# Per-head rows of a mixer-and-experts layer spread over the partitions by broadcast transfers instead of one-hot products

## The reference, cut to what matters

```
# mLSTM, 4 heads: causal weights from a cumulated gate row b and an input gate row
D = where(causal, b[..., :, None] - b[..., None, :] + ig[..., None, :], -inf)
m_t = maximum(inter, max(D, -1)); Dw = exp(D - m_t[..., None]); iw = exp(inter - m_t)
# gated delta rule, 8 heads: a decay row gc and a factor row beta
gc  = cumsum(g, -1)
gam = exp(where(causal, gc[..., :, None] - gc[..., None, :], -inf))
a_mat = where(strict, beta[..., :, None] * gam * einsum('bhcld,bhcsd->bhcls', k, k), 0)
sol = triangular_solve(eye + a_mat, rhs);  p = gam * einsum(q, k)
qg  = q * exp(gc)[..., None]
```

## Time and profile before

| what | value |
|---|---|
| three runs | 1386.42, 1386.41, 1384.55 us, median 1386.41 us |
| the profiled execution's own time | 1386.72 us |
| its span in the trace | 1384.9 us |
| TensorE busy | 1309.3 us, 95% of the span |
| VectorE busy | 334.1 us, 24% |
| ScalarE busy | 178.0 us, 13% |
| moved by DMA | 460.64 MB, mean 333 GB/s |

### The profile page before, as it was taken

How to read it: one execution, slowest core, us unless ns; L and a number is a source line. 1 busy time by engine, 2 the same in 40 slices (tenths; PEclk the granted TensorE clock), 3 DMA queues, 4 the chain that set the end, 5 groups by cost and what they waited for, 6 DMA issues and landing times.

```text
span 1384.9 us, 18396 instructions
## 1 busy us (share of the span) xinstructions
PE 1309.3 (95%) x7510; PEld 710.6 (51%) x7510; DVE 334.1 (24%) x724; ACT 178.0 (13%) x271; POOL 9.7 (1%) x17
## 2 busy tenths in 40 slices
PE   7999999999999999999999989899998989989895
PEld 6888888888886443443433324233332423333241
DVE  3847473122133111112011020110201011020113
ACT  1331622011001100101000100010010001001000
POOL 0110000000000000000000000000000000000000
PEclk9999999999999999999999999999999999999998
DMA  6533323323796999999999999999999999999995
GB/s 234 182 122 107 110 81 116 128 87 133 296 352 231 370 421 421 422 422 422 422 421 422 421 422 422 422 422 422 422 421 422 421 422 422 422 422 422 422 422 209
DMA packets 72274, 460.64 MB, mean 333 GB/s; under 512 B 14096, under 2 KB 14736, under 8 KB 17584
## 3 DMA queue, kind: packets, MB, share of 16 engines
q1 hardware_dynamic: 65824, 455.24, 80.9%
q10 hardware_dynamic: 6416, 4.93, 1.2%
HBM read 458.70 MB, written 1.44 MB: 332 GB/s over the span
## 4 chain that ended last, share of the span: by engine, by line
PE 57%; SPq 21%; DMA 18%; DVE 3%; issue 2%; ACT 0%; DVEq 0%
SPq L369 21%; PE ps L483 19%; PE ps L832 16%; DMA mix<-expert_w 10%; DMA ring<-expert_w 6%; PE ps L850 4%; PE ps L501 3%; PE ps L789 3%; PE ps L777 3%; PE ps L825 3%; PE ps L724 2%; PE ps L493 1%; DMA ring<-small_w 1%; DMA mix<-x_turned 1%; DMA mix<-stream_w 1%
## 5 line engine op out<-in xcount | busy, mean ns | idle before, releaser
L832 PE MATMUL ps<-ring,mix 128*64 128x512 f32 x1536 | 343.1, 592 | 2.5 <-DMA ring<-expert_w 2.5
L483 PE MATMUL ps<-mix 128*128 128x256 f32 x1248 | 273.7, 380 | 2.2 <-DVE ring L1423 2.2
L483 PEld LDWEIGHTS ps<-mix 128*128 128x128 f32 x1248 | 235.9, 190 | 35.7 <-issue 4.1
L832 PEld LDWEIGHTS ps<-ring,mix 128*64 128x64 f32 x1536 | 108.6, 137 | 210.3 <-issue 192.5
L850 PE MATMUL ps<-ring,mix 128*64 128x512 f32 x768 | 181.2, 599 | 31.6 <-DMA ring<-expert_w 31.6
L1662 DVE TENSOR_SCALAR mix<-ps 128x512 f32<-128x512 f32 x32 | 22.1, 692 | 539.6 <-PE ps L832 539.6
L850 PEld LDWEIGHTS ps<-ring,mix 128*64 128x64 f32 x768 | 50.4, 136 | 149.1 <-issue 83.4
L832 PE MATMUL ps<-mix 128*64 128x512 f32 x512 | 116.4, 593 | 2.1 <-DMA mix<-expert_w 2.1
L1671 DVE COPY mix<-ps 128x512 f32<-128x512 f32 x32 | 22.1, 692 | 239.2 <-PE ps L841 239.2
L850 PE MATMUL ps<-mix 128*64 128x512 f32 x256 | 60.6, 601 | 12.5 <-DMA mix<-expert_w 12.5
L789 PEld LDWEIGHTS ps<-mix 128*64 128x64 f32 x1088 | 63.9, 142 | 11.0 <-issue 9.1
(11 more groups left out here) (254 smaller groups left out, 780.0 us busy)
## 6 DMA issues: line engine op xcount, KB each, us to landing
ring<-expert_w SPq DMA_DIRECT2D x288, 1024.0 KB, 26.5
mix<-expert_w SPq DMA_DIRECT2D x96, 1024.0 KB, 26.8
mix<-stream_w SPq DMA_DIRECT2D x42, 1024.0 KB, 4.8
mix<-stream_w SPq DMA_DIRECT2D x10, 512.0 KB, 4.1
mix<-x_turned SPq DMA_DIRECT2D x2, 512.0 KB, 5.9
mix<-planes ACTq DMA_DIRECT2D x1, 1024.0 KB, 9.6
mix<-x SPq DMA_DIRECT2D x2, 512.0 KB, 6.1
mix<-ln_g ACTq DMA_DIRECT2D x2, 512.0 KB, 6.3
```

The costliest lines, as they stand in the source:

```text
L483: ins = mm(o[:, m * S:(m + 1) * S], w[:, c, m * P:(m + 1) * P], rhs[:, c, :], start=(m == 0 and c == 0), stop=(c == nk - 1), skip_group_ch ...
L832: ins = mm(PS[64 * a:64 * a + 64, bank + g, :], XE[j][:, c, 64 * a:64 * a + 64], w[:, a * D + g * 512:a * D + g * 512 + 512], start=False, ...
```

## The change

The one-hot products bb, gb, gr and mr go. Three DRAM tensors are added: `rows_gb` (2 x 8 x 256), `rows_gt` (2 x 8 x 128) and `rows_m` (4 x 3 x 128). SP writes the rows there in five transfers behind the load of lx0, and reads them back, each spread over 64 or 128 partitions, in four transfers behind the load of lx1 (`EG` in two of 256 KB, `GAM` 1 MB, `ME` 768 KB) and two behind the load of ly0 (`KB`, 512 KB in all). DVE and ACT then work in place on `EG`, `KB`, `GAM` and `ME` in SBUF, where they read PSUM before. DVE multiplies KB in two instructions instead of four. The banks of later projections shift by two places in the rotation of four. The order of everything else stays.

```diff
-FILL = (("mq", "mk", "mr0", "mr1", "lg"), ...
+FILL = (("mq", "mk", "lg"), ...
...
+                if name == "lx0":
+                    sp.wait_ge(E("rows_ready"), 1)
+                    sp.wait_ge(E("rows_ready_act"), 3)
+                    sp.dma_start(rows_gb[0], RW[64:64 + GH]).then_inc(E("rows_out"), 16)
+                    sp.dma_start(rows_gb[1], RW[96:96 + GH]).then_inc(E("rows_out"), 16)
+                    sp.dma_start(rows_gt.rearrange("t h l -> h t l"), RW[64:64 + GH].rearrange("h (t l) -> h t l", t=NT)
+                                 ).then_inc(E("rows_out"), 16)
+                    sp.dma_start(rows_m[:, 0:2, :], NM[0:MH].rearrange("h (b l) -> h b l", b=2)
+                                 ).then_inc(E("rows_out"), 16)
+                    sp.dma_start(rows_m[:, 2, :], NM[0:MH, P:2 * P]).then_inc(E("rows_out"), 16)
+                if name == "lx1":
+                    sp.wait_ge(E("rows_out"), 80)
+                    for a in range(2):
+                        sp.dma_start(EG[64 * a:64 * a + 64], rows_gb[0].rearrange("(j a) s -> a j s", a=2)[a]
+                                     .partition_broadcast(64)).then_inc(E("eg_in"), 16)
+                    sp.dma_start(GAM, rows_gt.rearrange("t h l -> (t h l)").rearrange("(n q) -> n q", n=4)
+                                 .partition_broadcast(P)).then_inc(E("gam_in"), 16)
+                    sp.dma_start(ME, rows_m.partition_broadcast(P)).then_inc(E("me_in"), 16)
+                if name == "ly0":
+                    sp.wait_ge(E("gsilu"), 1)
+                    for a in range(2):
+                        sp.dma_start(KB[64 * a:64 * a + 64, :, a, :], rows_gb[1].rearrange("(j a) s -> a j s", a=2)[a]
+                                     .partition_broadcast(64)).then_inc(E("beta_in"), 16)
...  (TensorE: the loops for bb, gb, gr and mr are taken out)
...  (ScalarE)
-                full(act, f"gb{n}")
-                A(EG[:, 2 * n:2 * n + 2, :], ps(f"gb{n}").rearrange("p (c s) -> p c s", s=S), ACT.Exp
-                  ).then_inc(free(f"gb{n}"), 1)
+                act.wait_ge(E("eg_in"), 32)
+                A(EG[:, 2 * n:2 * n + 2, :], EG[:, 2 * n:2 * n + 2, :], ACT.Exp).then_inc(E("eg"), 1)
...  (VectorE)
-                    ins = tt(KB[h, 2 * n:2 * n + 2, a, :], ps(f"bb{n}")[h].rearrange("p (c s) -> p c s", s=S),
-                             KT[h, 2 * n:2 * n + 2, :], ALU.mult)
+            dve.wait_ge(E("beta_in"), 32)
+                step(tt(KB[h, :, a, :], KB[h, :, a, :], KT[h], ALU.mult))
...
+            dve.wait_ge(E("eg"), 2)
...
+            dve.wait_ge(E("gam_in"), 16)
+                    gam = GAM[:, 2 * t + h // 4, (h % 4) * P:(h % 4 + 1) * P]
+                    ins = stt(gam, gam, RC[:, t, 0, 64 + h:65 + h], CM[:, K_GTRI], ALU.subtract, ALU.add)
+                    if h % 4 == 3:
                         ins.then_inc(E("gam_arg"), 1)
...
+                dve.wait_ge(E("me_in"), 16)
+                        stt(ME[:, h, 0, :], ME[:, h, 0, :], RC[:, 0, 0, h:h + 1], CM[:, K_MTRI], ALU.add, ALU.add)
+                        ts(ME[:, h, 1, :], ME[:, h, 1, :], RC[:, 0, 0, h:h + 1], None, ALU.add)
```

More of the change, by code:

```diff
@@ L102 @@
 NB16 = P // BS
[L103 removed]
+FILL = (("mq", "mk", "lg"), ("ms00", "ms10", "ms01", "ms11", "mv0"), ("mv1",), ("mo0", "mn"),
         ("mo1", "gz0", "mt", "gz1"), ("ga00",))
@@ L145, in bank_uses @@
     p("lx2", "lx3")
-    order += [("bb0", 4), ("bb1", 5), ("gb0", 6), ("gb1", 7)]
     p("ly0")
     order += [("vt0", 4), ("vt1", 5), ("kt0", 6), ("kt1", 7)]
-    order += [(f"gr{n}", 4 + n) for n in range(4)]
     p("ly1")
@@ L343, in layer_kernel @@
         blocks = nc.dram_tensor("blocks", (3, NB16, P // NB16, BS, BS), F32, kind="Internal").ap()
+        rows_gb = nc.dram_tensor("rows_gb", (2, GH, S), F32, kind="Internal").ap()
+        rows_gt = nc.dram_tensor("rows_gt", (NT, GH, P), F32, kind="Internal").ap()
+        rows_m = nc.dram_tensor("rows_m", (MH, 3, P), F32, kind="Internal").ap()
         def diagonal(buf, g):
@@ L537, in _ @@
                 proj(f"lx{n}")
[L539 to L554, removed]
             proj("ly0")
@@ L561, in _ @@
                 many(f"kt{t}", [(j * P, j * P + P, KT[:, j, t * P:(t + 1) * P], ident) for j in range(GP)])
-            for n in range(4):
-                many(f"gr{n}", [(m * S, m * S + S, ident[:, 64 + 2 * n + m:65 + 2 * n + m].to_broadcast([P, P]), RW)
-                                for m in range(2)])
             proj("ly1")
@@ L584, in fill @@
                             many(f"lg{b}", [(k * S, k * S + S, w[:, k, b, :], XA[:, b, :]) for k in range(2)])
[L585 to L590, removed]
                     elif name[:2] == "ms":
@@ L1265, in _ @@
             dve.sem_inc(E("khat"), 1)
[L1266 to L1269, removed]
-                    ins = tt(KB[h, 2 * n:2 * n + 2, a, :], ps(f"bb{n}")[h].rearrange("p (c s) -> p c s", s=S),
-                             KT[h, 2 * n:2 * n + 2, :], ALU.mult)
-                ins.then_inc(free(f"bb{n}"), 1)
-                dve.wait_ge(free(f"bb{n}"), uses[f"bb{n}"][1])
+            dve.wait_ge(E("beta_in"), 32)
+            for a in range(2):
+                h = slice(64 * a, 64 * a + 64)
+                step(tt(KB[h, :, a, :], KB[h, :, a, :], KT[h], ALU.mult))
             dve.sem_inc(E("kb_ready"), 1)
@@ L1280, in _ @@
             conv_lru(1)
-            for n in range(2):
-                moved(dve, f"gb{n}")
+            dve.wait_ge(E("eg"), 2)
             for a in range(2):
@@ L1302, in _ @@
                 dve.wait_ge(free(f"kt{t}"), uses[f"kt{t}"][1])
+            dve.wait_ge(E("gam_in"), 16)
             for t in range(NT):
                 for h in range(GH):
[L1306 to L1313, removed]
+                    gam = GAM[:, 2 * t + h // 4, (h % 4) * P:(h % 4 + 1) * P]
+                    ins = stt(gam, gam, RC[:, t, 0, 64 + h:65 + h], CM[:, K_GTRI], ALU.subtract, ALU.add)
+                    if h % 4 == 3:
                         ins.then_inc(E("gam_arg"), 1)
-            for n in range(4):
-                dve.wait_ge(free(f"gr{n}"), uses[f"gr{n}"][1])
-            dve.sem_inc(E("gam_arg"), 2)
             plane4 = lambda k: CM[:, k].unsqueeze(1).to_broadcast([P, 4, P])
@@ L1383, in mlstm_exponents @@
             def mlstm_exponents():
+                dve.wait_ge(E("me_in"), 16)
                 for n in range(2):
[L1386 to L1392, removed]
+                    for h in (2 * n, 2 * n + 1):
+                        stt(ME[:, h, 0, :], ME[:, h, 0, :], RC[:, 0, 0, h:h + 1], CM[:, K_MTRI], ALU.add, ALU.add)
+                        ts(ME[:, h, 1, :], ME[:, h, 1, :], RC[:, 0, 0, h:h + 1], None, ALU.add)
+                        ins = stt(ME[:, h, 2, :], ME[:, h, 2, :], RC[:, 1, 0, h:h + 1], CM[:, K_MTRI], ALU.add,
                                   ALU.add)
-                    ins.then_inc(free(f"mr{n}"), 1)
-                    moved(dve, f"mr{n}")
-                    dve.sem_inc(E("me_arg"), 1)
+                    ins.then_inc(E("me_arg"), 1)
             def mlstm_scores():
```

## The result

The changed kernel takes 1376.93 us in the median of 4 runs (1376.16 to 1378.57), the kernel before 1385.79 us in 4 (1384.55 to 1386.42): 0.9938 of the time, 95% interval 0.9925 to 0.995. Forecast were 1378.1 us and the range 1376.0 to 1382.0. The profiled execution took 1376.41 us, its span is 1374.6 us, 10.3 us less than before; its DMA moved 463.56 MB.

What follows compares the result with a forecast made beforehand. TensorE bounds the product stages and DMA the expert stage, in series; the change touches only the first. 3.60 + 4.08 + 0.65 = 8.33 us off, giving 1378.1 us, range 1376.0 to 1382.0.

Steps and rivals of the forecast that it cites:

- bb and gb: Between lx3 and ly0 on TensorE: ly0 waits for none of these products' readers, so all 3.60 us go.
- VectorE next: KB to QG before BV: KB must begin by 82.8, its rows land by 79.2; hidden, 3.6 us to spare.
- gr: Between kt and ly1 on TensorE: ly1 uses a projection bank, so 4.08 us go, more than the products' own time.
- GAM's margin: Before the first AT: GAM's last exp at about 104.5, AT readable at 105.55; about one microsecond left.
- mr: Between mk and y4: removing the products gains 0.65 us, bounds 0 and 2.2; ScalarE's tanh and table load hold lg.
- rival A: At lg behind mk: ScalarE does not hold lg, mr gives its full 2.2 us; 1376.5 us; chance 0.04.
- SP's queue: Loads behind the spreading transfers: at 414 GB/s lx2's load lands at 64.3, needed at 73.07; slack 8.8 us.
- The expert stage: Expert chunks behind the mixers: the DMA-bound stage begins earlier by what TensorE gains and keeps its length.
- Rival D: Before lx2: slow spreading transfers hold the stream in SP's queue; at 50 GB/s 24 us more, 1410 us; chance 0.05.
- Rival C: In the expert stage: DMA sets the pace and the gain is swallowed; 1386 us; chance 0.06.
- Rival E: At lg4 to y4: a new 1.3 us wait halves TensorE's clock, 7.2 us more; 1385.3 us; chance 0.02.

## Why the prediction was right, step by step

**bb and gb**, 3.60 forecast, 3.80 measured. The mechanism is right; the missing 0.20 lies at the borders. Between lx3 and bb and again between ly0 and kt the old order has 0.1 us more than an unbroken run of projections (13.91 and 7.01 where 13.81 and 6.91 stand in the rhythm of 20.72 / 3). I had read starts only and taken ly0's start in the new order as bb's in the old.

**VectorE next.** KB was to have landed by 79.2; its later half, issued at 69.9, landed at 76.2, just before its factor KT was ready at 77.06. VectorE began KB at 77.20 without a wait, 5.6 us ahead of the latest start that the forecast allowed (82.8). One statement was wrong: EG's exps, done at 88.68, were not ahead of QG. VectorE stood 1.45 us for them, and 1.06 us before QB. It cost nothing, since it then stood 3.44 us for vt and began BV at 94.92, where the forecast had vt's first bank full at 94.9.

**gr**, 4.08 forecast, 4.10 measured. The sum was right and its division was not quite: 0.6 us were waits that the removal of bb and gb takes away by itself.

**GAM's margin** was put at 1 us. The first AT was multiplied at 105.30 (forecast 105.55). GAM's last quarter was ready at 104.24, ahead even of the first AT. The 16 instructions took 4.29 us from SBUF, against 4.23 from PSUM before and 4.38 in the run with gr: the value taken was right, and the far bound (twice the time) far off.

**mr**, 0.65 forecast, 0.61 measured, for the reason given, and rival A (2.2 us in full) is refuted by the pair of kernels with the tanh moved, in which it comes true.

**SP's queue.** lx2's landing was forecast for 64.3 and came at 66.4. Two terms were mis-sized. The DMA view of 48 to 56 us, slices of 0.2 us:

```profile
GB/s 0 0 0 0 0 123 205 0 164 205 82 328 410 492 410 410 492 369 451 369 410 353 87 307 353 297 271 266 271 271 256 400 389 82 287 328 328 369 410 451
```

First the start: I had let the bytes flow at the full rate from 48.7, and up to 50.0 only 0.14 MB moved: 1.0 us is lost there. Second the rate of the spreading transfers with rows of 1 KB: from 52.2 to 55.0, where EG's rows go, 0.78 MB moved, 278 GB/s, and at 414 that would have taken 0.9 us less. The two make 1.9 of the 2.1 us. EG's two transfers, 256 KB each, landed 5.8 and 6.3 us after issue, KB's two 6.0 and 6.3. The changed kernel's DMA view of 68 to 80 us, slices of 0.3 us: the run of 437 is ly0's load, what follows up to 171 is mostly KB's rows, at about 200 to 310.

```profile
GB/s 27 0 0 0 0 0 218 0 191 191 437 437 437 437 437 437 300 297 314 215 205 232 259 171 27 0 0 0 0 0 0 0 0 0 0 0 0 0 0 27
```

Those with rows of 6 and 8 KB ran at the full rate, 415 GB/s from 56 to 64 us. Whether the short rows or the 64 partitions make the others slower no run separates. Rival D had the right mechanism, order in the queue, but feared rates under 163 GB/s, where the slowest stretch here has 278; the run with 4 MB more is D come true in the small. The order that the Trainium skill states ("DMA: Bandwidth & Descriptors", "Queues, rings and completion order") agrees with that run: the landing at 76.5 us is that of a load which lets every spreading transfer pass first.

**The expert stage** kept its length: from the first product of line 832 to the last of line 777 it is 928.52 and 928.87 us in the profiles of before, 928.39 and 928.84 in those of the changed kernel. Rival C is refuted.

**The clock.** Rival E did not come true where I put it: no profile shows half clock behind the 1.18 us wait at lg4. But my evidence against it was one lucky execution. I argued that the clock stays up behind a wait of 2.18 us, since the profile of before showed 1.00 there; the second profile of the same kernel shows 0.50. The Trainium skill's rule ("TensorE: Matmul & The Clock Gate", "Why this matters for your kernels") is that idle gaps between bursts take the clock back to half. It names a longer gap than the 2.18 us behind which the clock fell here in five of ten profiles; the traces agree with the rule behind the 3.22 us and show that a shorter wait can be enough. Nor does the length of a wait decide alone. I had called the gap before mo1 the shorter one, beside the router's waits; it is the longer one. In the router stage the clock falls to 0.50 in all twelve profiles, and the waits ahead of it are of 0.8 and 1.3 us, with short products between them. From the first profile of before:

```profile
424.22 2.05 PE L501 MATMUL ps<-mix 128*128 128x128 f32 x16 [1.28 <-DVEq L1602]
...
429.57 0.41 PE L767 MATMUL ps<-mix 128*128 128x32 f32 x2 [0.81 <-DVEq L1616]
```

**The measured difference** of 8.9 us is 0.5 over the forecast 8.3: 0.2 are the borders, and the rest is less than the medians can tell (0.9925 to 0.995 of the time is 6.9 to 10.4 us). The profiled executions differ by 10.3 us, and of that 1.6 us are chance, the wait for stream_w and the place of the half clock in the router stage.

## What to carry to other kernels

Where one engine is without a gap and the next stage's start hangs on it, work taken off it counts in full, but only up to the next reader: look at who empties the banks behind the removed work before you book its time. A transfer that is ready long before it is used is free until the queue's next load becomes late; work that point out from the bytes queued ahead of it. And take two profiles before booking a difference of one or two microseconds to a change: here a wait on DMA and a fall of the clock came and went with the execution.

## What the runs showed of the hardware that was not expected

- TensorE's granted clock fell to 1.2 GHz behind a wait of 2.18 us in five of ten profiled executions, which are of eight kernels, at a cost of 1.7 us each time: from y4 to the out-projection the five take 234.86 to 234.89 us, the other five 233.20 to 233.59. Behind a wait of 3.22 us it fell as well (1.8 us). Behind waits of 1.1 to 1.8 us in the mixers it fell in none of twelve profiles, in the router stage, with waits of 0.8 and 1.3 us, in all twelve.
- Spreading rows of 1 KB from DRAM over 64 partitions moved at about 200 to 310 GB/s (278 in the mean over EG's); rows of 6 and 8 KB over 128 partitions at about 415.
- VectorE's fused operation on 128x128 float32 took the same time with its first operand in SBUF as in PSUM (4.29 against 4.23 and 4.38 us for 16).
- A projection directly behind products with 64-column weights took 7.17 us instead of 7.07 (ly0 behind gb). The start of bb behind lx3 came 0.1 us late too; that it is the width of the weights and not something else in them is not shown.
